# A two-block transformer kernel on one core: the first block's mixer for all 512 tokens at once

## Chip, cores and metric

One core of a Trainium2 chip runs the whole program. The metric is device microseconds per execution; lower is better. Everything is float32. A float32 matmul shows in the trace as two records of TensorE (two passes), each with a weight load of its own.

## The reference, cut

512 tokens of width 1024 pass two blocks. Only the first concerns the change, and of it the mixer and the expert layer:

```python
h = rmsnorm(x, norm_mix_g); proj = h @ w_in
cb, cc, cx, q, k, v, gc, ga = split(proj, 8 x 1024 columns)
y_conv = (cb * causal_depthwise_conv3(cc * cx)) @ w_conv_out
y_attn = diff_attention(q, k, v, rel_bias, lam) @ w_attn_out   # 8 heads, two softmaxes a head, causal
x = x + (sigmoid(gc) * y_conv + sigmoid(ga) * y_attn) @ w_mix_out
x = x + cross_attention(rmsnorm(x), rmsnorm(mem), w_cq, w_ckv, w_co)
hf = rmsnorm(x)
# 8 heads; 2 x 128 sub-keys a head, the best 16 of the 256 sums: 128 experts a token
act = gelu(einsum('td,thkd->thk', hf, peer_u[experts]))
x = x + einsum('thk,thkd->td', softmax(scores) * act, peer_v[experts])
```

The second block (NSA attention, gated MLP, a convolution, cross-attention, a feed-forward layer of width 2816) is computed as before.

## The kernel before

**Halves and tiles.** Tokens are handled in two halves of 256 (h = 0, 1), a half in two tiles of 128 (t = 0 to 3). Weights come in chunks of 512 KB through a ring of six buffers (`RING`), loaded by SyncE's queue (L636) when the chunk six earlier is used up. A projection is either transposed (`proj_T`: 8 chunks of 8 products, the 128 columns of a weight block stationary, 256 tokens streaming, L771 and L772) or by token (`proj_tok`: 8 chunks of 4 products, a tile stationary, 512 weight columns streaming, L791 and L792). Sites carry names: cc, cx, cb, cv, gc, q, k, v, ga, ya, mx are the mixer; mk, mv the keys and values of the memory; cq, co cross-attention; pq the expert queries; qn to zc, ou, xq, xo, up, down the second block.

**Experts.** For each token tile 128 gathers are made: gather c brings, for each of 128 tokens, the row `uv` of its c-th expert, U and V together, 2048 floats a token. Gathers are indirect DMAs issued by GpSimd (L2004) into 8 slots. Per gather VectorE takes the dot product of U with the token (L1783), ScalarE applies gelu (L1293) and the gate (L1297 or L1300), and the scaled V row is summed: by VectorE onto X (`add`, L1763), or, for the gathers listed in `pe_sums`, by TensorE, which multiplies a diagonal matrix (made by ScalarE at L1305) with V into two PSUM banks held for that (L1030, L1031). A slot is free once its V row is summed. Before the gathers of a tile can be issued, VectorE has to choose the experts (`choices`: the steps top, cand, pick, gates; four parts of 32 gathers a tile), from scores that TensorE makes out of pq (`scores`, L888).

**Order of the work.** `Plan` writes one list of steps, and each engine executes its part of the list in order. `first_a` comes first: `mixer_0` (half 0), `cross_0`, `experts(0)`. Then `weave` interleaves three generators by a clock of planned costs, always letting the one with the lowest clock go on: `work` (scores of half 0; the mixer of half 1; cross-attention of half 1; scores of half 1; the second memory; then, when gain 1 has been passed and tile 3 is chosen, `second(0)`, the whole second block for half 0), `peers` (the 512 gathers, 2.55 a gather; one waits until its part is chosen) and `choices`. A chunk is planned at 3.4, an attention step of half 1 at 9.0, of cross-attention at 4.0, of NSA at 8.0. A gather goes on TensorE only while `self.light` is set, which is during the attention steps, and then two in three. Last comes `second(1)`, alone. With `lean`, as in all of `work`, ScalarE makes all plain evictions of PSUM.

**The mixer by halves.** `mixer_0` projects 256 tokens, runs `da` (16 units of a head and a query block, in 20 steps) woven with the chunks of mk and half of mv, and then spills: keys, values and the bias matrix go to `head_scratch`, the memory's keys and values to `kv_scratch`. Half 1 reads all eleven sites' weights again, in the gather stage, fetches `head_scratch` head by head for its `da`, and reads `kv_scratch` back for its cross-attention. One step of `da` for unit u: TensorE makes two logit tiles; VectorE adds the bias and takes the maximum (L1563) and negates it (L1605); ScalarE takes exp with its sum (L1191); VectorE takes reciprocals (L1577) and lambda (L1580); POOL (half 0, L1976) or ScalarE (half 1, L1183) scales one softmax; VectorE combines (L1582); TensorE transposes it and multiplies with v (L827, L843); ScalarE evicts both (L1202, L1208).

## Time and profile before

| | us |
|---|---|
| median of 3 runs (lowest, highest) | 3117.09 (3110.16, 3132.23) |
| profiled execution, its time | 3107.55 |
| its span, first to last instruction | 3105.8 |
| TensorE busy | 2470.5 (80%) |
| VectorE busy | 1845.0 (59%) |
| ScalarE busy | 1113.9 (36%) |
| GpSimd busy | 720.2 (23%) |
| DMA moved | 827.07 MB, 266 GB/s over the span; 536.90 MB of it by the gathers |
| mean granted TensorE clock | 0.873 of full speed |

How to read it: busy time is a sum over stages that differ. An engine that is at 80% of the span can be the bound in one stage and wait in the next, so the stretches have to be looked at one by one. Full speed of TensorE's clock is 2.4 GHz; 0.5 is 1.2 GHz.

### The profile page before, as it was taken

How to read it: one execution, taken by the hardware profiler on the slowest of the kernel's cores; microseconds unless marked ns; L12 is line 12 of the kernel's file. 1: busy time of each engine (PE TensorE's matmuls, PEld its weight loads, DVE VectorE, ACT ScalarE, POOL GpSimd, SP SyncE). 2: the span in 40 equal slices, each digit the busy share in tenths (PEclk: the TensorE clock that was granted, in tenths of full speed). 3: DMA queues.
4: the chain of work that ended last, by engine and by line, in shares of the span. 5: the costliest groups of instructions: out<-in, count | busy, mean ns of one | idle time of the engine just before them, and what ended most of it. 6: DMA issues, size and time to landing. Idle time of an engine off the chain costs nothing.

```text
span 3105.8 us, 29103 instructions
## 1 busy us (share of the span) xinstructions
PE 2470.5 (80%) x9858; PEld 1773.2 (57%) x9858; DVE 1845.0 (59%) x4351; ACT 1113.9 (36%) x2709; POOL 720.2 (23%) x584
## 2 busy tenths in 40 slices
PE   7999898875946777688580988768887979978998
PEld 6885665764833336455450774445675358745883
DVE  2101311799998777676888759868799514622430
ACT  2101212231423775263222348646455113422220
POOL 0000000222345444241212425525333101100110
PEclk9999799887978988899785958889999985789999
DMA  6544243779999999997865979979999641022453
GB/s 206 165 153 156 69 156 115 297 306 343 401 412 411 403 399 380 419 417 269 344 217 203 365 293 347 371 298 410 409 417 418 274 155 62 1 83 82 154 151 120
DMA packets 156644, 827.07 MB, mean 266 GB/s; under 512 B 16920, under 2 KB 20392, under 8 KB 90704
## 3 DMA queue, kind: packets, MB, share of 16 engines
q0 software_dynamic: 73728, 536.90, 42.9%
q1 hardware_dynamic: 78144, 276.21, 25.4%
q10 hardware_dynamic: 4624, 12.11, 1.1%
q8 instruction: 78, 1.28, 0.2%
q14 instruction: 70, 0.57, 0.1%
HBM read 816.74 MB, written 8.41 MB: 266 GB/s over the span
## 4 chain that ended last, share of the span: by engine, by line
PE 44%; DVE 27%; ACT 12%; DMA 9%; issue 6%; POOL 1%; ACTq 0%; DVEq 0%; SPq 0%
PE ps L771 19%; DVE X L1763 8%; DMA BIG<-in_uv,BIG 7%; DVE BIG L1783 7%; PE ps L1008 5%; PE ps L791 4%; PE ps L792 4%; PE ps L772 3%; ACT L1293 2%; DVE BIG L1694 2%; PE ps L912 2%; DVE BIG L1691 1%; ACT WK L1075 1%; PE ps L980 1%; PE ps L959 1%
## 5 line engine op out<-in xcount | busy, mean ns | idle before, releaser
L2004 POOL DMA_INDIRECT BIG<-in_uv,BIG x512 | 658.5, 1286 | 1429.8 <-DVE X L1763 857.7
L771 PE MATMUL ps<-BIG,RING 128*128 128x256 f32 x3472 | 821.4, 390 | 95.2 <-ACT BIG L1120 39.3
L771 PEld LDWEIGHTS ps<-BIG,RING 128*128 128x128 f32 x3472 | 677.0, 196 | 203.9 <-ACT BIG L1120 40.9
L1783 DVE CUSTOM_DVE_ANT_0 BIG<-BIG 128x1024 f32<-128x1024 f32 x512 | 619.6, 1218 | 83.9 <-DMA BIG<-in_uv,BIG 82.8
L1763 DVE SCALAR_TENSOR_TENSOR X<-BIG,small,X 128x1024 f32<-128x1024 f32 x398 | 509.7, 1281 | 71.3 <-ACT small L1297 70.9
L1293 ACT ACTIVATE small<-small 128x1 f32<-128x1 f32 x512 | 102.8, 201 | 775.7 <-DVE small L1783 774.1
L771 PE MATMUL ps<-WK,RING 128*128 128x256 f32 x1232 | 283.0, 381 | 21.4 <-DVE BIG L1543 19.4
L771 PEld LDWEIGHTS ps<-WK,RING 128*128 128x128 f32 x1232 | 231.8, 190 | 62.6 <-DVE BIG L1543 29.8
L791 PE MATMUL ps<-RING,BIG 128*128 128x512 f32 (+1 forms) x448 | 227.2, 589 | 17.5 <-DVE BIG L1522 8.8
L792 PE MATMUL ps<-RING,BIG 128*128 128x512 f32 (+1 forms) x448 | 225.9, 586 | 0.0
L1120 ACT ACTIVATE BIG<-ps 128x256 f32<-128x256 f32 (+2 forms) x143 | 55.9, 395 | 357.9 <-PE ps L772 312.4
L1481 DVE TENSOR_SCALAR BIG<-ps 128x256 f32<-128x256 f32 (+2 forms) x37 | 16.8, 454 | 258.8 <-PE ps L772 206.6
L759 PE MATMUL ps<-ident,BIG 128*128 128x128 f32 x128 | 51.1, 405 | 145.5 <-ACT BIG L1091 65.9
L1008 PE MATMUL ps<-RING,BIG 128*128 128x512 f32 x352 | 155.7, 604 | 9.8 <-DVE BIG L1543 9.8
L1474 DVE TENSOR_TENSOR X<-ps,X 128x512 f32<-128x512 f32 x40 | 27.2, 689 | 213.0 <-PE ps L792 126.4
L1293 ACT ACT_TABLE_LOAD x119 | 152.7, 1283 | 2.1
L791 PEld LDWEIGHTS ps<-RING,BIG 128*128 128x128 f32 x448 | 85.7, 194 | 116.7 <-issue 93.3
L772 PE MATMUL ps<-BIG,RING 128*128 128x256 f32 x496 | 147.5, 379 | 0.0
L792 PEld LDWEIGHTS ps<-RING,BIG 128*128 128x128 f32 x448 | 86.3, 193 | 103.2 <-issue 101.7
L1075 ACT ACTIVATE WK<-X 128x1024 f32<-128x1024 f32 x32 | 33.7, 1054 | 273.2 <-DVE X L1474 250.8
L1008 PEld LDWEIGHTS ps<-RING,BIG 128*128 128x128 f32 x352 | 67.7, 193 | 96.8 <-issue 83.8
L1297 ACT ACTIVATE small<-small,BIG 128x1 f32<-128x1 f32 x398 | 117.3, 295 | 12.9
(260 smaller groups left out, 3145.7 us busy)
## 6 DMA issues: line engine op xcount, KB each, us to landing
RING<-in_w_up SPq DMA_DIRECT2D x88, 512.0 KB, 4.3
RING<-in_w_down SPq DMA_DIRECT2D x44, 512.0 KB, 4.1
RING<-in_w_pq SPq DMA_DIRECT2D x32, 512.0 KB, 3.5
RING<-in_w_cc SPq DMA_DIRECT2D x16, 512.0 KB, 8.7
RING<-in_w_cx SPq DMA_DIRECT2D x16, 512.0 KB, 4.3
RING<-in_w_cb SPq DMA_DIRECT2D x16, 512.0 KB, 5.5
RING<-in_w_cv SPq DMA_DIRECT2D x16, 512.0 KB, 4.3
RING<-in_w_gc SPq DMA_DIRECT2D x16, 512.0 KB, 5.7
```

Of the source, the lines that this page charges most:

```text
L771: e.matmul(ps[:, 0:256], W[:, j, :], src[:, j, 0:256], start=j == 0, stop=False)
L772: e.matmul(ps[:, 0:256], W[:, 7, :], src[:, 7, 0:256], start=False, stop=True).then_inc(pe.sem, pe("mm", site, h, c, m))
L791: e.matmul(ps[:, 0:n], src[:, 2 * j, t * 128:(t + 1) * 128], W[:, 0, :], start=j == 0, stop=False)
L792: mm = e.matmul(ps[:, 0:n], src[:, 2 * j + 1, t * 128:(t + 1) * 128], W[:, 1, :], start=False, stop=j == 3)
L912: mm = e.matmul(ps[pr, 0:nn], W1[l // 16][:, l % 16, :], KN[pr, s, f0:f0 + 16 * nn - 15:16], start=l == 0, stop=l == 31)
L1008: mm = e.matmul(ps[:, :], AF[:, f, t * 128:(t + 1) * 128], W[:, hh * 512:(hh + 1) * 512], start=f == 0, stop=f == 21)
L1075: e.activation(SQ[:, 0:width], src(i), ACT.Square, accum_out=small[:, o + i:o + i + 1]).then_inc(act.sem, act("sq", key, i))
L1293: e.activation(a, dots[:, k % 8:k % 8 + 1], ACT.Gelu).then_inc(act.sem, act("gelu", k))
L1297: e.activation(a, a, ACT.Copy, scale=GS[:, t, c:c + 1]).then_inc(gate.sem, gate("gate", k))
L1763: e.scalar_tensor_tensor(out=X[:, t, :], in0=slot[k % NS][:, 1024:2048], scalar=acts[:, k % 8:k % 8 + 1], in1=X[:, t, :], op0=ALU.mult, op ...
L1783: e.tensor_tensor_reduce(out=u, in0=HF[:, t % 2, :], in1=u, scale=1.0, scalar=0.0, op0=ALU.mult, op1=ALU.add, accum_out=dots[:, k % 8:k % ...
L2004: e.indirect_dma_start(out=slot[i], out_offset=None, in_=I["uv"], in_offset=bass.IndirectOffsetOnAxis(ap=IDX[:, t, c:c + 1], axis=0)).then ...
```

## The change

The mixer runs once for 512 tokens in `first_a`, ahead of every gather. Its transposed projections stream 512 columns instead of 256; v is still done by halves (its weights are read twice), mx too (half 1 in `cross_0`, in the place where half of mv stood). `da` has 32 units in 36 steps, woven with all chunks of mk and mv at doubled planned cost. Both norms of the mixer come first. The spills to `head_scratch` and `kv_scratch` and their loads are gone; buffers move. In `da` the bias and q are stored negated, so that VectorE's fused add and minimum yields the negated maximum that exp needs, and one product of three scalars and one combination take the place of the scaling of one softmax on POOL; the reciprocal of the first sum is applied when ScalarE evicts the result. The pace of choices becomes (1.0, 2.5, 2.5, 2.5). Every V row of tiles 0 and 1 is summed by TensorE; tiles 2 and 3 keep the rule with `light`.

```diff
-    def mixer_0(self):
-        yield from self.norm(("mix", 0), False)
+    def mixer(self):
+
+        yield 0, "norm", ("mix", 0)
         yield 0, "prepare"
+        yield 0, "norm", ("mix", 1)
         yield 0, "mem_in", 1
+        for h in range(2):
+            for k in range(8):
+                yield 0, "trans", ("mix", h), k, False
...
-        yield from self.proj_tok("v", 0, 2, False)
-        yield 0, "mark", ("da", 0)
+        for h in range(2):
+            yield from self.proj_tok("v", h, 2, False)
+        yield 0, "mark", "da"
+
+        def da():
+            for i in range(36):
+                yield 3.0, "da", i
 
         def memory():
             yield from self.proj_T("mk", 1, 2, False)
-            yield from self.proj_tok("mv", 1, 1, False)
-
-        yield from ((0,) + step for step in weave(self.da(0), memory()))
...
+            yield from self.proj_tok("mv", 1, 2, False)
+
+        yield from ((0,) + step for step in weave(da(), ((2 * cost, *step) for cost, *step in memory())))
...
-        for k in range(8):
-            yield 0, "trans", ("o", 0), k, False
+        for h in range(2):
+            for k in range(8):
+                yield 0, "trans", ("o", h), k, False
         yield from self.proj_T("ya", 0, 2, False)
         yield from self.proj_tok("mx", 0, 2, False)
 
     def cross_0(self):
         yield 0, "mark", ("x", 1, 0)
         yield 0, "norm", ("x", 1, 0)
-        yield from self.proj_tok("mv", 1, 2, False, 1)
+        yield from self.proj_tok("mx", 1, 2, False)
...
     def work(self):
         yield from self.scores(0, True)
-        yield 0, "mark", "b"
-        for step in self.mixer(1):
-            while step[1:3] == ("chunk", "k") and (1, 3) not in self.chosen:
-                yield "wait"
-            yield step
-        yield 0, "mark", "kv"
-        yield 0, "kv_in"
         yield from self.cross(1, 1, True)
         self.reached.add("x1")
         yield from self.experts(1, True)
         yield from self.scores(1, True)
+        while (1, 3) not in self.chosen:
+            yield "wait"
         yield from self.memory(2, True)
...
-                yield from self.choose(t, p, (1.0, 3.0, 0.5, 0.5)[t])
+                yield from self.choose(t, p, (1.0, 2.5, 2.5, 2.5)[t])
...
                 late.append(k)
-                if self.light:
+                if t < 2:
+                    self.pe_sums[t].append(k)
+                elif self.light:
...
+                n = src.shape[2]
                 for j in range(7):
-                    e.matmul(ps[:, 0:256], W[:, j, :], src[:, j, 0:256], start=j == 0, stop=False)
-                e.matmul(ps[:, 0:256], W[:, 7, :], src[:, 7, 0:256], start=False, stop=True).then_inc(
+                    e.matmul(ps[:, 0:n], W[:, j, :], src[:, j, :], start=j == 0, stop=False)
+                e.matmul(ps[:, 0:n], W[:, 7, :], src[:, 7, :], start=False, stop=True).then_inc(
                     pe.sem, pe("mm", site, h, c, m))
...
-                    e.tensor_tensor(small[:, o + 8:o + 9], small[:, o + 7:o + 8], nlam, ALU.mult).then_inc(dve.sem, dve("da2", h, u))
-                    w.wait_ge(*at["da3", h, u])
-                    e.scalar_tensor_tensor(out=L0_, in0=L0_, scalar=small[:, o + 3:o + 4], in1=L1_, op0=ALU.mult,
-                                           op1=ALU.add).then_inc(dve.sem, dve("dp", h, u))
+                    e.scalar_tensor_tensor(out=small[:, o + 8:o + 9], in0=small[:, o + 7:o + 8], scalar=small[:, o + 2:o + 3], in1=nlam,
+                                           op0=ALU.mult, op1=ALU.mult).then_inc(dve.sem, dve("da2", u))
+                    own()
+                    e.scalar_tensor_tensor(out=P0, in0=P1, scalar=small[:, o + 8:o + 9], in1=P0, op0=ALU.mult,
+                                           op1=ALU.add).then_inc(dve.sem, dve("dp", u))
...
-                        add_max(banks[ps_of["dl", h, u, c]][:, 0:nk], bias, WK[:, 2 * (u % 3) + c, :], nk, o, "dl", h, u, c)
-                        e.tensor_scalar(small[:, o + 1:o + 2], small[:, o:o + 1], -1.0, None, ALU.mult).then_inc(
-                            dve.sem, dve("dneg", h, u, c))
...
             def total(t):
                 w.wait_ge(*at["sum", 128 * t + 127])
                 w.wait_ge(acc.sem, acc.n)
+                w.wait_ge(*at["ev", "co", t // 2, 1, t % 2])
...
-            def da(h, i):
-                u = i - 2
-                if h == 0 and 0 <= u < 16:
...
-                    e.tensor_scalar(L, L, small[:, o + 8:o + 9], None, ALU.mult).then_inc(pool.sem, pool("da3", h, u))
...
-                    w.wait_ge(*at["kv_st"])
```

## Rows read from the trace of the kernel before

**Rows 1.** Busy time by stage: engines with records, clock, DMA share, GB/s.

```profile
core 0: us, PE busy (x) PEld busy (x) DVE busy (x) ACT busy (x) POOL busy (x), PEclk, DMA share, GB/s
541.90:1694.10 1152.20, 784.21 (x3000) 563.17 (x3000) 949.83 (x2142) 459.86 (x1121) 371.62 (x299) 0.84 0.88 349
1694.10:2460.00 765.90, 627.34 (x2541) 426.98 (x2542) 602.04 (x1214) 404.88 (x994) 286.83 (x214) 0.87 0.92 369
2460.00:3105.80 645.80, 564.48 (x2340) 412.76 (x2338) 190.89 (x668) 154.30 (x358) 45.85 (x40) 0.86 0.31 98
0.00:541.90 541.90, 494.46 (x1978) 370.32 (x1979) 102.22 (x328) 94.86 (x238) 15.87 (x32) 0.95 0.45 145
```

**Rows 2.** Waits from 541 to 1700 us: total us, times, longest.

```profile
POOL BIG L2004 <- DVE X L1763: 525.6, 193, 18.0
...
PE ps L888 <- ACT BIG L1120: 59.5, 8, 15.3
```

**Rows 3.** The chain that ended last: start us, us, what.

```profile
125.55 3.02 PE ps L771 x14
129.00 3.02 PE ps L771 x14
...
575.51 6.82 DMA BIG<-in_uv,BIG
...
3019.47 75.55 PE ps L1008 x176
```

**Rows 4.** Two stretches of all engines; then three of L2004 (gather issues) alone.

```profile
1250.00:1300.00 50.00, 34.47 (x87) 16.81 (x85) 40.81 (x56) 9.42 (x33) 18.33 (x16) 0.90 1.02 420
2250.00:2400.00 150.00, 121.63 (x520) 96.15 (x518) 142.19 (x248) 87.66 (x173) 49.44 (x45) 0.98 1.02 417
...
541.90:1694.10 1152.20, 371.62 (x299) 0.84 0.88 349
1694.10:2460.00 765.90, 286.83 (x214) 0.87 0.92 369
...
541.90:651.70 109.80, 21.73 (x20) 0.81 0.73 282
```

**Rows 5.** Attention: half 0's stretch; groups by shape in half 1's, 960 to 1130.

```profile
257.00:345.40 88.40, 75.79 (x294) 51.81 (x293) 28.08 (x150) 25.95 (x101) 12.23 (x16) 0.80 0.32 101
...
L1563 DVE CUSTOM_DVE_ANT_0 WK<-ps,BIG 128x512 f32<-128x512 f32 x14 | 9.5, 682 | 0.0
...
L1582 DVE SCALAR_TENSOR_TENSOR WK<-WK,small 128x512 f32<-128x512 f32 x6 | 4.5, 752 | 6.2 <-ACT WK L1183 6.2
...
L1191 ACT ACTIVATE WK<-WK,small 128x512 f32<-128x512 f32 x14 | 10.1, 722 | 1.3 <-DVE small L1605 1.3
```

**Rows 6.** Costs per gathered row: groups (busy us, mean ns), TensorE's timeline.

```profile
L1783 DVE CUSTOM_DVE_ANT_0 BIG<-BIG 128x1024 f32<-128x1024 f32 x512 | 619.6, 1218 | 83.9 <-DMA BIG<-in_uv,BIG 82.8
L1763 DVE SCALAR_TENSOR_TENSOR X<-BIG,small,X 128x1024 f32<-128x1024 f32 x398 | 509.7, 1281 | 71.3 <-ACT small L1297 70.9
L1293 ACT ACTIVATE small<-small 128x1 f32<-128x1 f32 x512 | 102.8, 201 | 775.7 <-DVE small L1783 774.1
...
L1300 ACT ACTIVATE small<-small,BIG 128x1 f32<-128x1 f32 x114 | 33.6, 295 | 3.7
...
L1305 ACT ACTIVATE DG<-ident,small 128x128 f32<-128x128 f32 x58 | 23.3, 402 | 1.9
...
1102.74 1.02 PE L1030 MATMUL ps<-BIG,DG 128*128 128x512 f32 x2
...
1104.46 1.02 PE L1030 MATMUL ps<-BIG 128*128 128x512 f32 x2
```

**Rows 7.** The choices on VectorE: groups over the whole span.

```profile
L1694 DVE FIND_INDEX8 BIG<-BIG 128x8 uint32<-128x128 f32 (+1 forms) x192 | 61.0, 330 | 0.0
...
L1691 DVE MAX8 BIG<-BIG 128x8 f32<-128x128 f32 (+1 forms) x192 | 54.5, 325 | 20.5 <-ACT BIG L1281 20.2
...
L1725 DVE TENSOR_TENSOR BIG<-iota,BIG 128x512 f32<-128x512 f32 x32 | 22.2, 693 | 1.1
```

**Rows 8.** The chain at the start of the last stage.

```profile
2487.73 7.01 DMA BIG<-in_final_g
```

More of the change, by code:

```diff
@@ L292, in first_a @@
     def first_a(self):
-        yield from self.mixer_0()
+        yield from self.mixer()
         yield from self.cross_0()
@@ L468, in program @@
         ROOM = at_(W0 + 15360, 512)
-        DIAG = [DG[:, 0, :], DG[:, 1, :], at_(W0 + 15872, 128), at_(W0 + 16000, 128)]
+        DIAG = [at_(W0 + 15872 + 128 * i, 128) for i in range(4)]
         K0 = W0 + 4096
@@ L871, in cross @@
                         ps = bank("xv", layer, h, hd, d)
-                        if not (layer == 1 and h == 1):
-                            for t in range(2):
-                                w.wait_ge(*at["ev", "mv" if layer == 1 else "nv", layer, 1, t])
+                        for t in range(2):
+                            w.wait_ge(*at["ev", "mv" if layer == 1 else "nv", layer, 1, t])
                         w.wait_ge(*at["ev", "xt", layer, h, 2 * hd])
@@ L1173, in proj_tok, with da @@
                         e.activation(ZG[:, t, :], ps[:, :], ACT.Gelu_apprx_tanh).then_inc(act.sem, act("ev", site, h, c, t))
-            def da(h, i):
-                units = da_units(h)
-                u = i - 2
-                if h and 0 <= u < 16:
-                    nk = (units[u][1] + 1) * 128
-                    o = 80 + 10 * (u % 3)
-                    L = WK[:, 2 * (u % 3) + 1, 0:nk]
-                    w.wait_ge(*at["da2", h, u])
-                    e.activation(L, L, ACT.Copy, scale=small[:, o + 8:o + 9]).then_inc(act.sem, act("da3", h, u))
+            def da(i):
@@ L1204, in da @@
                 u = i - 4
[L1205 to L1220 removed]
+                if 0 <= u < 32:
+                    hd, qb = da_units[u]
+                    o = 80 + 10 * (u % 4)
+                    w.wait_ge(*at["mm", "dv", u])
+                    e.activation(o_tile(qb)[:, hd, :], banks[ps_of["dv", u]][:, 0:128], ACT.Copy, scale=small[:, o + 3:o + 4]).then_inc(
+                        act.sem, act("ev", "dv", u))
@@ L1222, in mem_in, with da_norm @@
+            def da_norm():
+                for q in ENGINES:
+                    w.wait_ge(*at["mark", "ms", q])
+                for qb in range(4):
+                    if qb >= 2:
+                        w.wait_ge(*at["dsum", qb - 2])
+                    e.activation(WK[:, 2 * (qb % 2):2 * (qb % 2) + 2, :].rearrange("p a (b d) -> p (a b) d", b=4), o_tile(qb),
+                                 ACT.Square).then_inc(act.sem, act("dsq", qb))
+                root(("o", 0), ms)
             def mem_in(tag):
@@ new lines, in da, with da_norm @@
+                        w.wait_ge(*at["mm", "dl", u, c])
+                        e.tensor_tensor_reduce(out=WK[:, 2 * (u % 3) + c, 0:nk], in0=banks[ps_of["dl", u, c]][:, 0:nk],
+                                               in1=RE[:, hd, (3 - qb) * 128:512], scale=1.0, scalar=3e38, op0=ALU.add, op1=ALU.min,
+                                               accum_out=small[:, o:o + 1]).then_inc(dve.sem, dve("ev", "dl", u, c))
+            def da_norm():
+                for qb in range(4):
+                    w.wait_ge(*at["dsq", qb])
+                    e.tensor_reduce(out=ms[:, 8 * qb:8 * qb + 8],
+                                    in_=WK[:, 2 * (qb % 2):2 * (qb % 2) + 2, :].rearrange("p a (b d) -> p (a b) d", b=4),
+                                    axis=AX.X, op=ALU.add).then_inc(dve.sem, dve("dsum", qb))
@@ L1624, in cross @@
+                w.wait_ge(*at["rstd", ("o", 0)])
+                for qb in range(4):
+                    v = o_tile(qb)
+                    e.tensor_tensor(v, v, ms[:, 8 * qb:8 * qb + 8].unsqueeze(2).to_broadcast([128, 8, 128]), ALU.mult).then_inc(
+                        dve.sem, dve("nrm", ("o", qb // 2), qb % 2))
             def cross(layer, h, i, lean):
```

344 lines of the change are left out of this document (111 added, 233 removed).

## Prediction, made before the change was run

> **What bounds the kernel now.** First the busy time, clock and DMA by stage [rows 1]. Four stages: the first half's mixer and cross-attention, 541.9 us, where TensorE is busy 494; the scores of tile 0 up to the start of the second block, 1152.2 us; the second block's first half beside the last gathers, 765.9 us; the second block's second half, 645.8 us. In the two middle stages nothing is full on average: TensorE 784 of 1152 and 627 of 766, VectorE 950 and 602, the DMA engines 0.88 and 0.92. The limit changes inside them. The waits tell by what: gathers (POOL L2004) stand 525.6 us for VectorE's sums L1763, that is for a free slot, and L888 waits 59.5 us for evictions that ScalarE holds in a queue behind the experts [rows 2].
>
> The granted clock in the first stage is 0.95, so TensorE's work is priced at 2.4 GHz. The chain of waits shows two steady 256-column chunks 3.45 us apart, and the 22 chunks of L1008 (176 records of 512 columns) in 75.55 us: 3.43 us each [rows 3]. A 512-column projection chunk has 16 such records: 6.87 us. Widening does not make a column cheaper; it saves only the second read of the weights.
>
> A gather brings 128 x 2048 floats, 1.05 MB; a chunk 0.52 MB. In 2250 to 2400 the DMA share is 1.02 at 417 GB/s [rows 4]. That prices a gather at 2.51 us and a chunk at 1.26 us at the least. 299 gathers are issued in the second stage and 214 in the third [rows 4].
>
> **Ahead of the gathers, term by term.** Cut into the first stage:
> - seven transposed sites (cc, cx, cb, cv, gc, q, k) and ga, ya go from 8 x 3.45 = 27.6 us to 8 x 6.87 = 54.9 us: 9 x 27.3 = 246 us. Their evictions double too, but stay far under 6.87 us a chunk.
> - v for the second half, 8 chunks of 3.43 us: 27.5 us; mx for the second half the same, 27.5 us; of mv, four chunks leave cross_0 for the attention stage: -13.7 us.
> - the second half's norm stands ahead of the first chunk: two squares, root, scale, 8 transposes. I take 7 us; 5 to 15 are possible, by the load of x2.
> - transposes and evictions of the second half of o: 8 us.
> - attention. Before: 16 units and 12 chunks took 88.4 us (257 to 345.4) [rows 5], with TensorE work of 12 x 3.45 = 41 plus 16 units of some 1.3 us (logits two times nk columns in two passes, transposes and values by blocks of 128, at 0.216 us per 256 columns): 62 us. So 26 us, or a factor 1.42, are coupling. Now: 32 units with nk 320 on average, 2.2 us each, 70 us, and 16 chunks, 55 us: 125 us. The loop VectorE, ScalarE, VectorE is shorter than that: for nk = 512 one L1563 0.68, two exponentials 0.72 with their reads, the scalars, one L1582 0.75 [rows 5], some 3.7 us, and 2.9 on average over the four lengths, 92 us; the POOL multiply and two negations a unit are gone. Between 125 + 26 = 151 and 125 x 1.42 = 178 I take 155, near the low end, since the fused loop gives TensorE more slack: +67 us. Floor 125 (+37).
>
> Sum: 246 + 41.3 + 7 + 8 + 67 = 369 us. The first score chunk starts at 911 instead of 541.9. Bounds 335 and 400. Nothing hides this: TensorE is the bound there, 494 of 541.9 us.
>
> What leaves the gather stage: 88 chunks, 304 us of TensorE and 88 x 1.26 = 111 us of DMA; 16 attention units; the spills through head_scratch and kv_scratch.
>
> **The sums of tiles 0 and 1.** A VectorE sum costs 1.28 us (L1763), beside a dot of 1.22 + 0.08 [rows 6]. On TensorE the two 512-column products with two passes repeat every 1.72 us (1102.74 to 1104.46) [rows 6], at full clock. ScalarE has 0.20 + 0.295 + 0.40 = 0.9 us per row [rows 6]. Of the 256 rows 60 went over TensorE before, so 196 move: 251 us off VectorE, 337 us onto TensorE.
>
> **Stage two, new.** The planner's clock says how many gathers stand beside which work: a gather is 2.55 units, a chunk 3.4. scores(0) 62 units, cross 102, scores(1) 62, memory 54: 281 units; the gathers run from 31 to 684. So 12 beside scores(0), 86 beside the rest of the work, 158 beside nothing but the choices of tiles 2 and 3.
> - scores(0) took 109.8 us before [rows 4], held by VectorE's choices; it loses some 14 sums there, TensorE gains 20 us. I take 105.
> - 86 gathers beside cross, scores(1), memory: TensorE 48 chunks 166, sums 86 x 1.72 = 148, and at 0.216 us a record scores 14 (64 records), cross 20 (64 and 16 transposes, rounded up), transposes of three norms 10: 358 us. DMA 86 x 2.51 + 48 x 1.26 = 276, VectorE 86 x 1.3 plus six or seven of the 16 choices. A choice is some 15 us: the searches L1691 54.5 and L1694 61.0, L1725 22.2 and two ops of its size, together 182 over 16 choices [rows 7], and some 4 for the replacing and the small ops that no row here shows; so 212 us. TensorE is the bound; with 25 us for the norms, during which the queue stands: 383. A gather takes 4.4 us here: the sums queue in order behind projection chunks and hold the slots.
> - 158 gathers alone: DMA 2.51, VectorE 1.3 + choices 0.6, TensorE 1.72, ScalarE 0.9. DMA is the bound: 2.6 x 158 = 411.
> - drain and total: 6.
>
> 905 us instead of 1152.2. Below, by DMA alone: 34 us to the first gather (before at 575.5 [rows 3]) + 256 x 2.51 + 66 x 1.26 = 760. Above, all 256 at 4.4: 1130.
>
> By the Trainium skill (DMA: Bandwidth & Descriptors, Where 436 GB/s comes from) a read from HBM is limited to some 358 GB/s per core, with the SBUF side at 435. By it a gather would be 2.93 us, and the last 158 would be 463 us, 52 more. The trace speaks against it: 417 GB/s over 150 us [rows 4]. The sum goes by the row.
>
> **Stage three, new.** Before, 219 gathers stood in the planner's order between its start and total(3), 765.9 us, and 41 units (12 chunks) of down came behind. Now second(0) starts with all 256 ahead: 219 as before, 765.9; 16 beside the last chunks of down, by DMA 16 x 2.51 + 12 x 1.26 = 55; 20 bare, on VectorE 1.3 + 1.28 each, 52. Sum 873.
>
> **Last stage.** From the load of final_g at 2487.7 [rows 8] to the end 3105.8 is 618 us, unchanged; the load now follows total(3) at once.
>
> 911 + 905 + 873 + 618 = 3307 us of span, with 1.75 us around it 3309 against 3107.55. The median shown, 3117.09, stands 9.5 over the profiled run; on it 3318. I say 3315, 6.4% slower.
>
> **Why so sure of the sign.** No change at all needs total(3) at 2488, so 1577 us from the first score chunk. The DMA engines alone need 34 + 512 x 2.51 + 176 x 1.26 = 1541. Before, a gather cost 765.9 / 214 = 3.58 us in stage three; break-even wants 3.0 over all 512.
>
> **Rivals.**
> 1. The DMA limit everywhere (other side). TensorE keeps up with sums beside projections and VectorE with choices, so that only DMA counts: 911 + 1541 + 618 = 3070 and some 8 us of drain: 3090 as a median; with the head's low bound 3055. It decides from a mean of 3.0 us a gather down. For it: share 1.02 in 2250 to 2400. Against: TensorE's demand in stage two's middle, 358 us for 86 gathers, and stage three, whose order is unchanged. 6%.
> 2. Stage two comes near its DMA bound, stage three not: 145 less, 3170; partly, 3230. 16%.
> 3. The clock. In the 411 us TensorE does 1.72 of 2.6 us. At 1.2 GHz a sum takes 3.43 us, and 158 of them 542 us: +131, 3446. Against: in 1250 to 1300 TensorE is busy 34.5 of 50 us at clock 0.90 [rows 4]. 8%. The Trainium skill (TensorE: Matmul & The Clock Gate, Part 1) says that the gate halves the clock of an array that was little busy; at 3.43 us the array would be full and the clock come back, so by page and row the loss is partial.
> 4. Slots: sums wait in TensorE's queue behind chunks so long that DMA starves, and VectorE's dots block ScalarE's evictions as in the L888 waits: 4.4 us for all: 905 becomes 1130, 3540. 4%.
> The forecast, 3250 to 3400, keeps 66%.
>
> Range 3165 to 3415: it takes in rival 2 and leaves 1 and most of 3 and 4, under 20%. A measurement tells about 1% from no change. Faster 0.03, same 0.05 (rival 1's two halves), slower 0.92.
>
> **What would show it.** w_pq's first chunk starts at 911 (880 to 940); gathers flow at 417 GB/s only once w_nv is in; TensorE has no gap in the stretch before; L1763 counts some 200; second(0) begins near 1816; total(3) near 2690. Wrong would be: the head grows by under 300 us, or the gathers beside cross and scores(1) pass at under 3 us each.

## The result and the profile after

| | before | after |
|---|---|---|
| median (lowest, highest) of 4 runs, us | 3124.66 (3110.16, 3136.87) | 3262.67 (3259.98, 3263.57) |
| profiled execution's time, its span | 3107.55, 3105.8 | 3259.98, 3258.1 |
| TensorE, VectorE, ScalarE, GpSimd busy, us | 2470.5, 1845.0, 1113.9, 720.2 | 2803.8, 1602.9, 1084.4, 662.8 |
| DMA moved | 827.07 MB | 776.65 MB |

The change makes the kernel slower: the ratio after to before is 1.0442, with an interval of 1.0390 to 1.0494. The prediction said slower, 3315 us or 6.4%; it is 3263 or 4.4%, inside the range. (The 3117.09 us that the prediction starts from is the median of three of the four runs of before.)

First the busy time by stage, the answer to [rows 1]. The rows are, in this order: two stretches of the head (which goes up to the first score chunk at 874.6); stage two, stage three and the last stage; three stretches of stage two.

```profile
core 0: us, PE busy (x) PEld busy (x) DVE busy (x) ACT busy (x) POOL busy (x), PEclk, DMA share, GB/s
25.60:483.00 457.40, 451.57 (x1059) 201.44 (x1060) 47.69 (x71) 31.70 (x51) 0.00 (x0) 0.99 0.26 86
...
483.00:609.30 126.30, 119.51 (x561) 76.19 (x560) 59.94 (x231) 62.28 (x198) 0.00 (x0) 0.96 0.21 70
...
874.60:1744.20 869.60, 742.86 (x2176) 394.38 (x2176) 559.56 (x1599) 359.36 (x987) 294.07 (x264) 0.97 0.91 360
1744.20:2618.00 873.80, 661.40 (x2584) 446.70 (x2584) 690.78 (x1327) 426.26 (x1072) 319.19 (x248) 0.82 0.92 371
2618.00:3258.10 640.10, 571.48 (x2300) 424.11 (x2300) 186.63 (x662) 151.69 (x353) 45.85 (x40) 0.83 0.29 92
...
874.60:968.90 94.30, 83.28 (x368) 64.36 (x369) 64.05 (x236) 35.86 (x81) 22.80 (x19) 0.97 0.81 317
968.90:1343.60 374.70, 347.60 (x1167) 218.15 (x1167) 209.93 (x644) 160.50 (x404) 93.16 (x84) 0.96 0.83 306
1343.60:1744.20 400.60, 311.98 (x644) 111.86 (x642) 285.58 (x723) 163.00 (x502) 178.11 (x161) 0.99 1.01 419
```

Set against [rows 1], the span's 152.3 us come from four differences: the head +332.7 (874.6 for 541.9), stage two -282.6 (869.6 for 1152.2), stage three +107.9 (873.8 for 765.9), the last stage -5.7 (counted in the kernel before from 2460.0; from its load of final_g at 2487.7, which is how the prediction counts, it is +22). The work that went ahead of the gathers costs 333 us there, and the gather stages give back 175.

Stage two has two parts with different limits. From 968.9 to 1343.6 TensorE is busy 347.6 of 374.7 us, and only 84 gathers are issued, one in 4.46 us. From 1343.6 to 1744.2 the DMA engines are full (1.01, 419 GB/s) and 161 gathers pass, one in 2.49 us. Call them the crowded and the bare stretch: beside the first run cross-attention, scores and memory projections, beside the second nothing but choices.

The waits from 875 to 1744 (total us, times, longest) answer [rows 2]:

```profile
POOL BIG L1898 <- PE ps L959: 524.3, 234, 23.7
...
DVE BIG L1687 <- DMA BIG<-in_uv,BIG: 168.1, 128, 5.3
```

The gathers (now L1898) stand 524.3 us for TensorE's sums L959. In the kernel before it was 525.6 us for VectorE's sums and, in the same window, another 141.8 for TensorE's:

```profile
POOL BIG L2004 <- PE ps L1031: 141.8, 49, 16.7
```

So the waits for a free slot fell from 667 to 524 us, in a stage that is 283 us shorter. The longest grew from 18.0 to 23.7 us. It stands across a norm: TensorE executes its list in order, and a sum behind the norm's transposes waits with them (start us, us, what, idle time before it):

```profile
1249.46 0.47 PE L703 MATMUL ps<-ident,BIG 128*128 128x128 f32 x1 [13.95 <-ACT BIG L1017]
1259.58 1.07 POOL L1898 DMA_INDIRECT BIG<-in_uv,BIG  x1 [23.75 <-PE ps L959]
```

The groups of lines, answering [rows 6]:

```profile
L1898 POOL DMA_INDIRECT BIG<-in_uv,BIG x512 | 613.3, 1198 | 1976.4 <-DVE BIG L1643 894.7
...
L1687 DVE CUSTOM_DVE_ANT_0 BIG<-BIG 128x1024 f32<-128x1024 f32 x512 | 621.2, 1219 | 215.9 <-DMA BIG<-in_uv,BIG 212.9
L958 PE MATMUL ps<-BIG 128*128 128x512 f32 x622 | 351.9, 649 | 101.0 <-ACT BIG L1217 94.2
...
L1666 DVE SCALAR_TENSOR_TENSOR X<-BIG,small,X 128x1024 f32<-128x1024 f32 x201 | 257.3, 1280 | 29.9 <-ACT small L1209 29.7
```

A dot still costs VectorE 1.22 us. Its sums (L1666) fell from 398 to 201, all in tiles 2 and 3, and TensorE has 311 sums (622 records of L958, two passes each).

The chain of waits in the head (start us, us, what) answers [rows 3]:

```profile
101.38 6.01 PE ps L715 x14
...
108.24 6.01 PE ps L715 x14
```

Two steady chunks of 512 columns stand 6.86 us apart, where the chunks of 256 stood 3.45 apart. The same weights for twice the tokens cost twice the time; TensorE gained nothing from the width.

### The profile page after: what moved, and what is told of

The parts are those of the page before. It is cut to its first block, busy times and chain, and to the rows that moved or that the text cites. A ratio compares the mean times of both kernels' runs of the same rounds, so it can differ in the third digit from the quotient of the medians.

```text
span 3258.1 us, 27751 instructions
## 1 busy us (share of the span) xinstructions
PE 2803.8 (86%) x9430; PEld 1680.2 (52%) x9430; DVE 1602.9 (49%) x4010; ACT 1084.4 (33%) x2756; POOL 662.8 (20%) x568
## 2 busy tenths in 40 slices
DMA packets 140669, 776.65 MB, mean 238 GB/s; under 512 B 15544, under 2 KB 15944, under 8 KB 74992
## 4 chain that ended last, share of the span: by engine, by line
PE 59%; DVE 14%; DMA 13%; ACT 10%; issue 3%; POOL 1%; ACTq 0%; DVEq 0%
PE ps L715 26%; DMA BIG<-in_uv,BIG 12%; PE ps L735 5%; PE ps L736 5%; DVE BIG L1687 4%; PE ps L716 4%; PE ps L958 3%; PE ps L959 3%; DVE X L1666 3%; PE ps L936 2%; PE ps L840 2%; ACT L1205 1%; PE ps L908 1%; PE ps L887 1%; ACT WK L1001 1%
## 5 line engine op out<-in xcount | busy, mean ns | idle before, releaser
L1898 POOL DMA_INDIRECT BIG<-in_uv,BIG x512 | 613.3, 1198 | 1976.4 <-DVE BIG L1643 894.7
L715 PE MATMUL ps<-BIG,RING 128*128 128x256 f32 (+1 forms) x2464 | 784.4, 470 | 11.3 <-ACT BIG L1026 4.1
L715 PEld LDWEIGHTS ps<-BIG,RING 128*128 128x128 f32 x2464 | 470.7, 192 | 309.9 <-issue 258.4
L958 PE MATMUL ps<-BIG 128*128 128x512 f32 x622 | 351.9, 649 | 101.0 <-ACT BIG L1217 94.2
L959 PE MATMUL ps<-BIG 128*128 128x512 f32 x622 | 330.1, 613 | 0.0
L715 PE MATMUL ps<-WK,RING 128*128 128x256 f32 x1232 | 292.5, 391 | 16.8 <-DVE BIG L1449 15.0
L1666 DVE SCALAR_TENSOR_TENSOR X<-BIG,small,X 128x1024 f32<-128x1024 f32 x201 | 257.3, 1280 | 29.9 <-ACT small L1209 29.7
L958 PEld LDWEIGHTS ps<-BIG 128*128 128x128 f32 x622 | 108.9, 198 | 265.6 <-ACT BIG L1217 214.5
L1040 ACT ACTIVATE BIG<-ps 128x256 f32<-128x256 f32 (+2 forms) x109 | 47.2, 434 | 555.1 <-PE ps L716 464.0
L959 PEld LDWEIGHTS ps<-BIG 128*128 128x128 f32 x622 | 123.4, 198 | 159.2 <-issue 159.2
L1393 DVE TENSOR_SCALAR BIG<-ps 128x512 f32<-128x512 f32 (+2 forms) x39 | 22.5, 577 | 370.8 <-PE ps L716 303.4
L736 PEld LDWEIGHTS ps<-RING,BIG 128*128 128x128 f32 x448 | 85.1, 190 | 101.0 <-issue 99.5
L735 PEld LDWEIGHTS ps<-RING,BIG 128*128 128x128 f32 x448 | 84.1, 190 | 100.7 <-issue 90.6
L716 PE MATMUL ps<-BIG,RING 128*128 128x256 f32 (+1 forms) x352 | 135.4, 466 | 0.0
```

The costliest lines, as they stand in the source:

```text
L715: e.matmul(ps[:, 0:n], W[:, j, :], src[:, j, :], start=j == 0, stop=False)
L716: e.matmul(ps[:, 0:n], W[:, 7, :], src[:, 7, :], start=False, stop=True).then_inc(pe.sem, pe("mm", site, h, c, m))
L735: e.matmul(ps[:, 0:n], src[:, 2 * j, t * 128:(t + 1) * 128], W[:, 0, :], start=j == 0, stop=False)
L736: mm = e.matmul(ps[:, 0:n], src[:, 2 * j + 1, t * 128:(t + 1) * 128], W[:, 1, :], start=False, stop=j == 3)
L958: e.matmul(banks[6][:, :], d, v[:, 0:512], start=first, stop=last)
L959: e.matmul(banks[7][:, :], d, v[:, 512:1024], start=first, stop=last).then_inc(pacc.sem, pacc("sum", k))
```

## Experiments

Four theories were to be told apart. A: the head's growth decides, since TensorE is the bound there and its work is only moved. B: the sums on TensorE are the cost. C: the gathers' bytes bound the bare stretch, so that nothing done to an engine helps there. D: the head grew less than forecast because attention is no longer bound by its own loop.

**The sum rule undone, layout kept.** From the changed kernel:

```diff
-                if t < 2:
-                    self.pe_sums[t].append(k)
-                elif self.light:
+                if self.light:
```

> The mixer for 512 tokens as changed, but tiles 0 and 1 go back to the rule of before: TensorE sums two of three V rows only while light is set (12 in cross-attention, some 105 while the work waits for tile 1), VectorE the other 139. Theory (TensorE is the bound beside cross, scores(1) and memory): that part of stage two falls from 374 us (968.9 to 1343) to 320 to 340, scores(0) grows by 5 to 10, the bare gathers stay at 2.49 us each by DMA; in all 20 to 40 us less than the changed kernel, near 3230. Rival (VectorE is the bound, and the sums on TensorE pay): 139 x 1.28 = 178 us more on VectorE show, stage two grows by 60 to 150, 3320 to 3410.

`light` is set during the attention steps and also, in both kernels, while the work waits ahead of `second(0)`. With the new layout that wait is the bare stretch, so the rule of before gives two in three of its sums to TensorE.

It takes 3236.91 us (3232.37 to 3238.61), ratio to before 1.0360 (1.0314 to 1.0407), 26 less than the changed kernel. Its crowded and bare stretches and 50 us of the bare one:

```profile
966.00:1293.60 327.60, 238.79 (x884) 170.86 (x884) 278.45 (x677) 141.11 (x340) 97.10 (x82) 0.86 0.86 334
1293.60:1718.40 424.80, 248.00 (x420) 86.68 (x420) 367.32 (x838) 143.95 (x456) 217.03 (x165) 0.86 1.00 409
...
1400.00:1450.00 50.00, 33.69 (x55) 11.66 (x53) 49.40 (x127) 20.15 (x57) 27.94 (x22) 0.83 0.99 402
```

The crowded stretch is 47 us shorter with the sums on VectorE, as TensorE's being its bound implies. The bare one is 24 us longer, which was not foreseen: VectorE is busy 49.4 of 50 us, the bytes fall to 402 GB/s, and a gather costs 2.57 us (424.8 / 165) where 2.49 was expected. So the new rule costs in one stretch and pays in the other. Layout and light rule alone are 113 us over the 3123.5 that the kernel before took on this chip: A holds. Of B, the sums, 26 us are left when they come on top of the new layout.

**The sums alone, layout of before.** From the kernel before:

```diff
-                if self.light:
+                if t < 2:
+                    self.pe_sums[t].append(k)
+                elif self.light:
```

> The kernel before with one part of the change alone: every V row of tiles 0 and 1 on TensorE, the mixer of half 1 still beside the gathers. Theory: TensorE gets 196 x 1.72 = 337 us in a stage where it has 368 us idle but most of it elsewhere than beside the projections; the projections with their gathers grow by 110, ga to mx by 40, co and pq by 20, scores(0) loses 15: 3107 + 100 to 160 = 3210 to 3270. Rival (the gathers' 525 us of waiting for VectorE's sums are the price, and TensorE's idle time takes the work): 50 to 150 us less than before, 2960 to 3060.

3215.61 us (3214.31 to 3245.46), ratio 1.0288 (1.0242 to 1.0334), 92 us more than before. The profile is of its longest run, 3245.46, whose last stage is of the longer kind told below (200.3 us for its NSA steps); the four others took 3214 to 3217. Stage two, and a stretch of it:

```profile
541.60:1806.30 1264.70, 1079.18 (x3784) 692.83 (x3784) 720.01 (x1946) 533.38 (x1316) 323.99 (x299) 0.93 0.84 318
...
651.00:900.00 249.00, 248.92 (x927) 175.70 (x927) 141.48 (x407) 94.74 (x234) 64.06 (x58) 1.00 0.92 333
```

With the second mixer still in the gather stage, TensorE is busy 248.92 of 249 us, and stage two grows by 112.5 us (1264.7 for 1152.2). There is no bare stretch in which the sums of tiles 0 and 1 could hide. The two parts of the change do not add: 92 alone and 113 alone would be 205, together they cost 138. With the layout of before the sums cost 92 us; with the new one they cost 47 beside the projections and give back 24 in the 400 us of the bare stretch.

**No sums for tiles 0 and 1; then also half of the bytes.** From the changed kernel, the V rows of these tiles are summed by neither engine, and a slot is free after the gate; the second kernel also gathers U alone. Both leave these rows out of x, so they serve only to time the rest. Of the code (the first cut is of both kernels):

```diff
-                    w.wait_ge(*at["sum", k - NS])
+                    w.wait_ge(*at["sum" if k - NS >= 256 else "gate", k - NS])
...
-                e.indirect_dma_start(out=slot[i], out_offset=None, in_=I["uv"],
+                e.indirect_dma_start(out=slot[i] if t >= 2 else slot[i][:, 0:1024], out_offset=None, in_=I["uv" if t >= 2 else "u"],
```

> The changed kernel without the sums of tiles 0 and 1: their V rows are gathered but not added to x; a slot is free when its gate is made. Theory: beside cross, scores(1) and memory DMA is the next bound, 86 x 2.51 + 48 x 1.26 = 276, so that part falls from 374 to 290 to 310; the bare gathers stay at 2.49 us, since DMA sets them; stage two 869 to about 785, total near 3175. Rival (the chain dot, gelu, gate, diagonal, sum holds the slots and sets the bare rate): the bare gathers come faster too, toward VectorE's 1.9 us, 300 instead of 401, total near 3080.

> As the changed kernel without the sums of tiles 0 and 1, and their 256 gathers bring the U row alone (512 KB instead of 1 MB). Theory (bytes through the DMA engines set the bare gathers at 2.49 us): they fall to VectorE's 1.3 + choices, 1.9 to 2.0 each, so the bare stretch from 385 to some 300 us, and the stretch beside cross and scores(1) from 312 to 250; total near 3030. Rival (the count of gathers, their issue on GpSimd or their latency over eight slots sets them): both stretches stay within 3%, total 3170.

They take 3173.12 and 3051.12 us, one run each. The two stretches of the first:

```profile
963.00:1250.40 287.40, 214.76 (x832) 159.51 (x832) 201.20 (x620) 132.72 (x327) 96.17 (x84) 0.85 0.95 387
1250.40:1660.50 410.10, 0.04 (x1) 0.00 (x0) 294.61 (x755) 100.67 (x346) 174.38 (x160) 0.51 1.01 421
```

and of the second:

```profile
966.00:1234.10 268.10, 216.31 (x826) 159.33 (x825) 210.01 (x645) 126.32 (x319) 99.75 (x84) 0.86 0.75 264
1234.10:1536.80 302.70, 0.00 (x0) 0.00 (x0) 275.05 (x714) 98.99 (x343) 196.76 (x159) 0.51 0.82 275
```

Without any sum the crowded stretch falls by 87 us, the bare one by nothing (410.1 for 400.6), at 421 GB/s for 419 and with TensorE idle: C. With half of the bytes the bare stretch falls by 107 us, and then VectorE is the next limit, 275.05 of 302.7. So in the bare stretch 2.5 us per gather is the price of its megabyte, and no rule of sums tried beats it.

**Attention without cover.** The memory's chunks are put behind it:

```diff
-        yield from ((0,) + step for step in weave(da(), ((2 * cost, *step) for cost, *step in memory())))
+        for part in (da(), memory()):
+            for step in part:
+                yield (0,) + step[1:]
```

> The changed kernel with the memory's projections behind the attention steps instead of woven in. Measured woven: 126 us. If the loop VectorE, ScalarE, VectorE sets a unit (2.9 us on average, 92 us, with ends 100): 100 + 55 = 155 us, 29 more, near 3290. If TensorE sets it also when alone (2.2 us a unit, 70 to 75 us): 130 us, and the total stays within 5 us of 3260.

3283.77 us, one run. Attention alone, then the memory's chunks:

```profile
483.00:575.00 92.00, 77.93 (x363) 50.38 (x360) 56.89 (x225) 57.88 (x191) 0.00 (x0) 0.79 0.02 6
575.00:635.00 60.00, 60.00 (x207) 39.55 (x207) 4.05 (x7) 5.24 (x10) 0.00 (x0) 0.98 0.43 140
```

Alone, 32 units take 92.0 us, 2.9 a unit: the loop's length that the prediction worked out, with TensorE's records filling 77.93 of it at a lower clock, 0.79. With the memory's 60 us behind them they need 152.0; woven they need 126.3, with TensorE busy 119.51. The 26 us are what the weave hides: woven evenly, the loop lies beside the chunks and the stage costs TensorE's work plus a few us. That is D. In the kernel before the 12 chunks ran out early. TensorE's last memory product there starts at 310.09; then the stage up to that product and behind it:

```profile
310.09 1.02 PE L792 MATMUL ps<-RING,BIG 128*128 128x512 f32 x2
...
257.00:311.10 54.10, 50.94 (x211) 34.50 (x209) 12.18 (x65) 12.15 (x43) 4.59 (x6) 0.97 0.49 156
...
311.10:345.40 34.30, 24.85 (x86) 17.32 (x86) 15.90 (x85) 13.81 (x58) 7.63 (x10) 0.54 0.05 16
```

In these last 34.3 us TensorE is idle 9.45 us and has a clock of 0.54; ahead of them it is idle 3.2 of 54.1 us, at 0.97. 36 of the 48 records of L843 (values) start there, those of 12 of the 16 units. At the prediction's price of 1.3 us a unit they are 16 us, so some 18 of the 26 us of coupling lie in this tail. Not told apart is how much of D comes from the even weave and how much from the shorter loop (no scaling on POOL, no negations): no run has the old loop under the new weave.

**The sums only where they are free.** From the changed kernel, tiles 0 and 1 use TensorE for every row while `light` is set, and VectorE elsewhere:

```diff
-                if t < 2:
+                if t < 2 and self.light:
                     self.pe_sums[t].append(k)
-                elif self.light:
+                elif t >= 2 and self.light:
```

> The changed kernel with tiles 0 and 1 summed by TensorE only while light is set, then every row: beside the projections VectorE sums, in cross-attention and the bare stretch TensorE. It takes the crowded stretch of the old rule (328 us instead of 375) and the bare stretch of the changed kernel (401 instead of 425): 3237 - 24 = 3213, and 50 below the changed kernel's 3263. Rival (the two stretches trade gathers, so that what one wins the other loses): 3237 or more. Either way above before, since the head is 333 us longer and DMA allows the gather stage no less than 1541.

3218.4 us (3201.06 to 3232.13), ratio 1.0329 (1.0271 to 1.0387):

```profile
966.00:1296.90 330.90, 250.54 (x911) 176.44 (x909) 273.14 (x673) 143.18 (x346) 98.11 (x82) 0.86 0.86 332
1296.90:1712.90 416.00, 307.27 (x629) 110.47 (x628) 309.32 (x786) 165.16 (x509) 179.59 (x165) 0.97 1.01 421
```

The crowded stretch is that of the old rule, and the bare one runs at the rate of bytes again (421 GB/s; 2.52 us for each of 165). Of the kernels with the new layout that sum every row it is the best, 44 us under the change and 105 over the 3113.49 of the kernel before on that chip. But the bare stretch takes 416.0 us where 401 was expected, and stage two ends at 1712.9: 31 us before the changed kernel's (1744.2), and only 5.5 before the old rule's (1718.4), where 24 were forecast. So most of the gain over the old rule did not come; that is nearer to the rival. The medians differ by more than the stages, because two of the four runs took 3201 and 3205 us and two 3232: in the profiled one, of 3204.74, the last stage is 24 us shorter with the same work (see below).

None of the rules of sums tried pays for the head; even without any sum of tiles 0 and 1 the kernel took 3173.12. The floor of bytes does not by itself forbid it, as the expectation has it: 874.6 + 1541 + 618 = 3034 us lie under the time of before.

**A part of the sums, layout of before.** The waits L2004 <- L1763 [rows 2] suggest that VectorE holds the gathers of the kernel before, so a quarter of its sums outside `light` was given to TensorE: in all tiles, then in tiles 0 and 1 alone. The first kernel, then the second:

```diff
+                elif k % 4 == 0:
+                    self.pe_sums[t].append(k)
...
+                elif t < 2 and k % 4 == 0:
+                    self.pe_sums[t].append(k)
```

> The kernel before, with every fourth V row that it sums on VectorE outside the attention steps given to TensorE instead. VectorE is busy 235 of 248 us beside the mixer's projections (651 to 900), TensorE 202, and a gather there costs 3.5 us; but DMA alone wants 2.51 + 0.94 there. Theory: the DMA engines are close behind, so at most 10 us are won, 3100 to 3125. Rival (VectorE is the bound of those stretches): 97 gathers x 0.3 us and the like in stage three, 30 to 50 us less, 3070 to 3090.

> The kernel before with every fourth V row outside the attention steps on TensorE, in tiles 0 and 1 only. With all four tiles stage two ended 10 us earlier (1688 against 1697.8) and stage three took 36 us more. Theory: the gain of stage two stays, stage three is as before: 5 to 15 us less than before, about 3108. Rival (what stage two wins, stage three gives back, since its gathers start with fewer rows in flight): within 5 us of before or above.

3159.06 us (3132.2 to 3161.5), ratio 1.0089 (1.0054 to 1.0124), and 3113.39 us (3102.66 to 3136.11), ratio 0.9987 (0.9955 to 1.0020). The first misses both its theory and its rival: it is slower. The second comes out as its rival said, within 5 us of before, for another reason than the rival's. Stage three, from one load of final_g to the next, of the first and of the kernel before in a second profile:

```profile
1688.00:2517.20 829.20, 701.51 (x2720) 461.59 (x2720) 567.66 (x1187) 423.21 (x1034) 274.48 (x213) 0.89 0.87 344
...
1697.80:2491.40 793.60, 647.41 (x2580) 435.82 (x2580) 607.93 (x1222) 408.72 (x1000) 287.30 (x214) 0.87 0.90 359
```

Stage two ends at 1688.0, where the two profiles of the kernel before have 1694.1 and 1697.8, and stage three takes 36 us more (829.2 for 793.6), with 54 us more of TensorE's work. Restricted to tiles 0 and 1 the loss is gone (stage three takes 793.8), but the gain with it: stage two ends at 1691.9, 2 or 6 us earlier, which is hardly more than the 3.7 us between two profiles of one kernel, and the time doesn't move. Half a millisecond of waits for one engine's sums did not mean that a quarter less of them is worth anything. What else holds the slots in the crowded part of that stage was not taken apart further.

**Another order, layout of before.** An attention step of half 1 is planned at 6.0 in place of 9.0; in the second kernel the pace of tile 1's choices is also 2.5 in place of 3.0.

```diff
-        yield from self.phase(True, (((5.0 if h == 0 else 9.0), "da", h, i) for i in range(20)))
+        yield from self.phase(True, (((5.0 if h == 0 else 6.0), "da", h, i) for i in range(20)))
...
-                yield from self.choose(t, p, (1.0, 3.0, 0.5, 0.5)[t])
+                yield from self.choose(t, p, (1.0, 2.5, 0.5, 0.5)[t])
```

> The kernel before with the planned cost of an attention step of half 1 at 6.0 instead of 9.0: 60 planner units less, so some 24 gathers move from beside the attention to behind it, and scores(1), which tile 2 waits for, come sooner against tile 1's gathers. In before 46 gathers were issued between 1420 and 1700, where DMA has room for 110. Theory (that hole is the waste of the order of before, the same gathers fill it): stage two 20 to 50 us shorter, total 3070 to 3100. Rival (TensorE and VectorE, not the order, set stage two): within 10 us of before.

> The same, and tile 1's choices at pace 2.5 as in the changed kernel, so that the chunk of k, which waits for them, is not held back. Theory: another 0 to 15 us less than with the step cost alone, if tile 1's choices hold the work; the same if they do not.

3127.13 us, ratio 1.0034 (1.0009 to 1.0058), and 3120.41 us, ratio 1.0012 (0.9984 to 1.0039). The first misses its theory, and its rival by 4 us: no gain. The second is 7 us under the first, within its "0 to 15", but that is inside the spread of either (30 and 41 us). Stage two up to the first load of the second block (final_g), then what follows up to 2480 or 2479, of the kernel before in its second profile:

```profile
541.90:1697.80 1155.90, 785.82 (x3000) 566.30 (x3000) 950.25 (x2142) 460.52 (x1121) 369.11 (x299) 0.84 0.88 348
1697.80:2480.00 782.20, 646.75 (x2579) 435.82 (x2580) 603.89 (x1217) 404.94 (x994) 287.30 (x214) 0.87 0.90 362
```

of the first:

```profile
541.90:1651.80 1109.90, 749.20 (x2930) 552.91 (x2928) 926.75 (x2107) 444.44 (x1069) 357.11 (x282) 0.83 0.88 346
1651.80:2479.00 827.20, 657.61 (x2580) 444.20 (x2580) 645.27 (x1271) 417.24 (x1034) 304.54 (x231) 0.84 0.91 364
```

and of the second:

```profile
541.90:1622.20 1080.30, 752.51 (x2935) 552.58 (x2933) 898.86 (x2071) 435.77 (x1045) 338.74 (x270) 0.85 0.87 344
1622.20:2479.00 856.80, 648.83 (x2584) 437.32 (x2584) 677.26 (x1312) 425.10 (x1064) 315.67 (x243) 0.84 0.92 372
```

Stage two ends 46 and 76 us earlier, but with 17 and 29 fewer gathers issued (282 and 270 for 299); the stretch behind has to issue 17 and 29 more. What is left of the gain at the start of the second block's second half shows in GpSimd's first operation there, L1966 (start us first), of the kernel before in its second and its first profile:

```profile
2505.30 3.40 POOL L1966 TENSOR_SCALAR WK<-X,small 128x1024 f32<-128x1024 f32 x1 [69.35 <-ACT small L1080]
...
2500.47 3.40 POOL L1966 TENSOR_SCALAR WK<-X,small 128x1024 f32<-128x1024 f32 x1 [69.62 <-ACT small L1080]
```

of the first kernel, with the last gather ahead of it:

```profile
2453.54 1.82 POOL L2004 DMA_INDIRECT BIG<-in_uv,BIG  x1 [0.66 <-DVE X L1763]
2495.20 3.40 POOL L1966 TENSOR_SCALAR WK<-X,small 128x1024 f32<-128x1024 f32 x1 [39.84 <-ACT small L1080]
```

and of the second:

```profile
2482.37 3.40 POOL L1966 TENSOR_SCALAR WK<-X,small 128x1024 f32<-128x1024 f32 x1 [28.02 <-ACT small L1080]
```

Against the second profile, of 46 us 10 are left, and of 76 23; against the first, whose stage two ends at 1694.1, of 42 us 5 and of 72 18. In the kernel before GpSimd stands 69 us there, its last gathers out long before; in the two others it stands 40 and 28, its last gathers being issued some 20 us later. A milestone that comes earlier because work was put behind it is little gain: count what it left.

The second kernel's profile, at 3089.14 us, is of its fastest run of 10 (up to 3129.83). Its last stage is of the shorter kind told below (176.7 us for its NSA steps at a clock of 0.64), as in the first profile of before, and the 18 us between the two are the whole difference in time (3107.55). The first kernel's is of the longer kind (200.6 us at 0.57), as in the second profile of before, and 10 us faster than it (3126.21 for 3136.15). So like against like both are somewhat faster in one execution each, and the medians do not show it. Whether these kernels fall into the longer kind more often, which would explain that, was not settled.

## Why the prediction held, and where its sum was off

The profiled span is 3258.1 where the sum said 3307. The 48.9 us are -36.4 in the head, -35.4 in stage two, +0.8 in stage three and +22.1 in the last stage.

**The head: +332.7, predicted +369.** The first chunk starts 8.1 us later for the second norm (7 predicted). From there to the end of v it takes 457.4 us; 56 chunks of 512 columns at 6.87 us and 16 of v at 3.43 are 439.6, and a rest of that size stood in the kernel before too (239.5 for 220.6). The step is +217.9, predicted 7 x 27.3 + 27.5 = 218.6. From ga to pq it is 265.3 for 196.5, +68.8, predicted 76.4. The growth lies just under the bounds that the prediction gave it, 335 and 400, and the first score chunk before its window of 880 to 940. The term that was mis-sized is "attention +67": 126.3 us for 88.4 is +38. Of "between 125 + 26 = 151 and 125 x 1.42 = 178 I take 155" the first number was right by itself. The 26 us of coupling were read as a property of attention and carried over. Some 18 of them belonged to the end of the stage, where the chunks had run out and the loop stood bare (the last 34.3 us in the experiment with attention alone); the change spreads the chunks over all 36 steps. The floor of 125, which the prediction named as a bound only, was the value. With the chunks put behind it the new attention costs 26 us more, so cover is worth that much here; that this is the number of before is chance, since then 32 units stand bare and not 12.

**Stage two: 869.6, predicted 905.** By parts 94.3 for 105, 374.7 for 383, 400.6 for 417 with the drain. The mechanism is as forecast: TensorE is the bound of the crowded stretch (sums removed, it falls by 87 us), DMA of the bare one (sums removed, nothing). The first part was over-priced by 11; why was not tested. The third was priced at 2.6 us a gather, a margin of 0.1 over the row of bytes, which the stretch didn't need: the chain of waits there consists of landings (start us, us, what) and GpSimd's timeline shows the issues 2.48 us apart:

```profile
1659.23 15.33 DMA BIG<-in_uv,BIG
...
1679.12 15.34 DMA BIG<-in_uv,BIG
```

```profile
1619.44 0.95 POOL L1898 DMA_INDIRECT BIG<-in_uv,BIG  x1 [1.54 <-PE ps L959]
1621.92 0.95 POOL L1898 DMA_INDIRECT BIG<-in_uv,BIG  x1 [1.54 <-PE ps L959]
```

Landings of one slot follow each other at 19.89 us, eight times 2.49: 15.3 us in flight, the rest the dot, the gate and the sum. The wait named is TensorE's sum, but the rate is that of the bytes, for the experiment without sums has the same one. The Trainium skill (DMA: Bandwidth & Descriptors, Where 436 GB/s comes from) has a read from HBM bound at some 358 GB/s per core, which it works out as half of what two cores share, and beside it notes 425 GB/s as measured for a transfer of 16 MB. With one core running, the trace does not agree with the bound and lies near the measurement: 419 GB/s over 400 us and 421 over 410.

**Stage three: 873.8, predicted 873.** The order is that of before with the chunks of down and bare gathers at its end, but that the sum meets is luck of two errors. TensorE's last product of down ends at 2529.7, 785.5 us into the stage, where the sum has 765.9 + 55 = 821; behind it the gathers stand bare for 88.3 us, where the sum has 20 gathers in 52:

```profile
2529.70:2618.00 88.30, 0.01 (x1) 0.00 (x0) 78.35 (x100) 19.99 (x67) 39.15 (x24) 0.52 0.94 386
```

There 24 gathers are issued and 8 more were in flight: 32 rows in 88.3 us, 2.76 each.

**The clock, rival 3, did not occur.** In the bare stretch TensorE is busy 311.98 of 400.6 us at a granted clock of 0.99, the 2.4 GHz level, with a pair of products for every gather. With no work at all, in the experiment without sums, the clock is 0.51, the 1.2 GHz level. The prediction also leaned on a full array bringing the clock back. No run shows that for sums, and the last stage speaks against relying on it: there TensorE is busy 20 of 20 us at 0.50, for 80 us on end (rows below).

**The other rivals.** Rival 1, the DMA bound everywhere, is ruled out by the crowded stretch at 4.46 us a gather and stage three at 3.5 (873.8 / 248). Rival 2 came in small part: stage two is 110 us over its DMA bound of 760, where the sum had 145 and the rival nothing. Rival 4 would have shown as 4.4 us for all gathers; it holds for 84.

**The last stage: 640.1, predicted 618.** It was taken as unchanged and its instructions are. The difference is 24 us in its NSA steps, of the changed kernel

```profile
2696.40:2896.80 200.40, 178.06 (x814) 141.63 (x813) 88.42 (x406) 75.76 (x201) 23.04 (x16) 0.56 0.06 22
```

and of the kernel before, in the execution that all rows ahead of the prediction come from

```profile
2569.80:2746.50 176.70, 154.08 (x814) 123.05 (x813) 88.27 (x406) 75.89 (x201) 23.05 (x16) 0.64 0.07 25
```

The same 814 records take 154 or 178 us of TensorE, at a mean clock of 0.64 or 0.56. In both executions the clock falls to 0.50 within the first 20 us of these steps. Then 20 us of each, 100 us behind the start of its row, of the kernel before and of the changed one:

```profile
2669.80:2689.80 20.00, 20.00 (x121) 16.25 (x120) 16.78 (x82) 13.73 (x37) 4.80 (x3) 0.93 0.00 1
...
2796.40:2816.40 20.00, 20.00 (x68) 15.12 (x67) 10.30 (x47) 8.30 (x25) 3.20 (x2) 0.50 0.00 0
```

In the one the clock has come back, in the other it stays at 0.50 for 40 us more, with TensorE busy all the time in both. Whether the change causes that was asked by profiling the unchanged kernel once more.

> The kernel before, profiled a second time. In its first profile the last stage's NSA steps took 179.6 us at clock 0.65, in the changed kernel 204 at 0.56, as in the three variants of it and in the sums alone. If that is chance of an execution, a second profile of before can show either, and its time moves with it by some 20 us. If the change causes it, it shows 180 again.

```profile
2572.70:2773.30 200.60, 176.85 (x814) 140.97 (x813) 88.41 (x406) 75.77 (x201) 23.05 (x16) 0.57 0.06 22
```

It took 3136.15 us (a span of 3134.4), and its NSA steps are the long ones. The kernel with sums while `light` has the short ones, with the change's layout:

```profile
2667.00:2843.60 176.60, 154.24 (x814) 123.09 (x813) 88.31 (x406) 75.85 (x201) 23.03 (x16) 0.64 0.07 25
```

So both lengths occur with either layout. The 24 us are no work of the change; all four runs of the changed kernel lie at 3260 to 3264, so whether it favours the long form was not settled. Long form against long form the change costs 3258.1 - 3134.4 = 123.7 us, the old rule of sums with the new layout 96 (3230.6) and the sums alone 109 (3243.5), one execution each. So each part alone costs about as much as the other, where the medians had 113 and 92; whichever comes second adds little, 28 us for the sums and 15 for the layout. Subtracting the 24, the errors of the sum are -36.4, -35.4, +0.8 and -2. So the total came closer than its parts: head and stage two were priced 72 us too high, and the long form, which nothing in the prediction has, hid 22 of them.

## What to carry to other kernels

Work that leaves a bandwidth-bound phase and goes ahead of it adds its full time there, and takes away no more than what the phase has above its floor of bytes; so work out that floor first (here 34 + 512 x 2.51 + 176 x 1.26 = 1541 us, against 1577 at which the change, with the head as forecast, would have broken even; it took 1743). A stage whose limits differ from stretch to stretch wants a rule by stretch: TensorE's sums cost 47 us beside projections and saved 24 beside choices alone, though the rule that took the better of the two ended stage two only 5.5 us before the old rule. When a stall is carried over to a changed loop, first ask where in the stage it stood; if only its uncovered end had it, better cover can remove it. When two executions are compared, first look for a stretch of the same instructions that took another time in each.

## What the runs showed of the hardware

- Two lengths of the same NSA steps: 176.6 and 176.7 us at a mean granted clock of 0.64, or 200.4 and 200.6 at 0.56 and 0.57, in different executions. That is some 24 us of 3110, and it may be why one kernel's runs fall into two groups (3132 to 3134, and 3147 to 3162, with a quarter of the sums moved; 3201 to 3205, and 3232, with sums while `light` is set), but only single executions were profiled, so that is not shown. A difference under 1% between two single profiles of this kernel has to be looked for there first.
- One core, running alone, read 419 to 421 GB/s by gathers of one megabyte for 400 us on end, at a DMA share of 1.01.
- The share of time that TensorE is busy does not tell its clock: 0.99 over 400.6 us at 78% busy (sums alone), 0.54 over 34.3 us at 72% (attention's tail), 0.50 over 20 us at 100% (NSA steps), and 0.51 in a stretch where it did nothing.
- A float32 product of 512 columns took the same per column as one of 256: 6.86 us for a chunk of 16 records of 512, 3.45 for 16 of 256.
